# Experts in pairs: two sorted groups of 64 tokens as fp32 products in the two halves of TensorE's output rows

## The chip, the core and the metric

The kernel runs on one core of a Trainium2 chip. The metric is the time on the device in microseconds (us), median of several executions.

## What is computed

Two transformer layers and a third block over 512 tokens of width 1024, all in float32. Only the mixture of experts of the last block matters here. Each token goes to 2 of 32 experts, so there are 1024 pairs of token and expert. An expert is a SwiGLU layer with 256 hidden columns:

```python
expert_id = g_sel[:, None] * EXPERTS_PER_GROUP + top_i        # 2 of 32 for each token
hid = silu(h @ w_gate[e]) * (h @ w_up[e])                      # (tokens, 1024) x (1024, 256), twice
y   = sum over the token's two experts of weight * (hid @ w_down[e])
```

With the inputs that the kernel gets, the reference sends between 5 and 67 pairs to an expert. Two experts get more than 64 (numbers 17 and 19, with 65 and 67), none gets more than 128.

A second, small part of the change is in the retention layer: there each head's output is centred (its mean over 128 columns is taken off) before it is normalised.

## The kernel before

The kernel is one hand-scheduled program: each engine has its own list of instructions and semaphores join them. TensorE's products are mostly split: an fp32 matrix is divided into a high part, rounded to the fp32r type, and a low remainder, and `three` (L585 to L587) issues three fp32r products for one product. ScalarE makes the high parts, VectorE subtracts to get the low ones.

The mixture of experts works on tokens sorted by expert. A routing stage ranks the pairs, and products with a selection matrix gather the 1024 sorted places into `xs` (L1242, L1257; copied out by ScalarE, L1896). Then 39 blocks of `SLOTS` = 128 places follow: 32 blocks, one for each expert, and `XOVER` = 7 more for experts with over 128 pairs, whose number is read from a table when the kernel runs. A block takes its window of 128 places out of `xs` at an address read from `window_at`, which an over block and the places behind an expert's last pair share with others: results of places that are not the block's are not stored.

One block `it` is, by engine:

- SP queue (L530 to L558): three panels of weights of 1 MB each, two for gate and up (`moe_raw`) and one for down (`moe_down`). The panels sit in 2 x 2 and 3 buffers, and a load waits until TensorE is done with the buffer (`up_done`, `down_done`).
- ScalarE (L1858 to L1919): high parts of the two up panels and of half the down panel (`high_up`, `high_down`), the window's high part (`high_window`), silu, the copy of the transposed hidden values, the copy of the result to `y_out`.
- VectorE (L2729 to L2751, loop from L2844): the low parts, and silu(gate) x up into `xhid` (L2852).
- TensorE (L1263 to L1314): `up(it)`: 8 x 3 split products, with the 128 tokens stationary and 512 columns of weights streaming; `down_moe(it - 1)`: two plain fp32 products (L1294) for half of the 256 hidden rows and 2 x 3 split ones for the other half; `turn_hid(it)`: two transposes. Block 0 takes its window from `xw0_hi` and `xw0_lo`, which is places 0 to 127 and needs no table.
- GpSimd (L2996 to L3000): an indirect DMA stores the 128 rows of a block to their sorted places in `expert_out` in HBM; rows that are not the block's are given an address past the end and dropped.

Behind the blocks GpSimd fetches each token's two results (`back`), and a last gated layer follows (panels `A_PG`), beginning on TensorE with the products of `w_ple` (L1322).

In the retention layer, a head's output goes to `ry` (L2548), `mean_r` (L1111 to L1113) makes its mean with a product by ones, and `centred` (L2550 to L2556) subtracts it.

## Time and profile before

| | |
|---|---|
| median of 3 runs | 2317.38 us (2317.13 to 2322.71) |
| profiled execution, its own time | 2318.59 us |
| its span in the trace | 2316.8 us |
| TensorE busy | 2270.3 us, 98% |
| VectorE, ScalarE, GpSimd busy | 1549.1, 1066.8, 185.8 us |
| moved by DMA | 308.86 MB, mean 133 GB/s |

The span is the time between the first and the last instruction of the core; the execution's own time is 1.8 us longer. A matmul's record in the trace covers its way through the array too, so that records overlap: what one costs in a row of them is the distance between their starts. An fp32 product has two records, each with its own load of the stationary operand (PEld rows). "Idle before" is time in which the engine did nothing, with what ended it.

### The profile page before, as it was taken

The numbers are of one execution on the slowest core, as the hardware profiler recorded it, in microseconds if no ns is written. First come the engines' busy times: TensorE is split into PE (matmuls) and PEld (weight loads), VectorE is DVE, ScalarE is ACT, GpSimd is POOL, SyncE is SP. The second block draws the span as 40 slices with busy tenths as digits, with TensorE's granted clock in tenths as the row PEclk, the third lists the DMA queues.
The fourth block names the chain that finished last, engine by engine and source line by source line (L and its number), as shares of the span: only waits on it lengthen the run. The fifth ranks groups of instructions, "written<-read, shape, count | busy, mean of one in ns | idle before, by whom it ended". The sixth has DMA issues, their size and how long they took to land. (4 is left out here: it accounts for less than half of the span.)

```text
span 2316.8 us, 28797 instructions
## 1 busy us (share of the span) xinstructions
PE 2270.3 (98%) x10880; PEld 1848.0 (80%) x10880; DVE 1549.1 (67%) x1948; ACT 1066.8 (46%) x1351; POOL 185.8 (8%) x158
## 2 busy tenths in 40 slices
PE   8999999999999999999999999999999999999998
PEld 6787888888779779998788888777788877777766
DVE  6776855555687676664655555777654678888868
ACT  5556522222334345653422222645422368888863
POOL 1334200000100000000000000200000101110120
PEclk9999999999999999999999999999999999999999
DMA  4322222222133531003322322111221349999961
GB/s 184 109 88 77 109 100 95 95 108 82 68 127 123 172 108 35 29 28 112 119 106 84 109 87 94 55 73 55 104 87 64 140 163 371 372 371 375 365 235 55
DMA packets 56662, 308.86 MB, mean 133 GB/s; under 512 B 10204, under 2 KB 10588, under 8 KB 26608
## 3 DMA queue, kind: packets, MB, share of 16 engines
q1 hardware_dynamic: 44336, 280.51, 32.3%
q0 software_dynamic: 10976, 24.22, 3.3%
q10 hardware_dynamic: 1248, 2.75, 0.3%
q8 instruction: 66, 1.08, 0.2%
q14 instruction: 36, 0.29, 0.0%
HBM read 294.64 MB, written 29.00 MB: 140 GB/s over the span
## 5 line engine op out<-in xcount | busy, mean ns | idle before, releaser
L585 PE MATMUL psum<-hn_hi,a_hi 128*128 128x512 f32 (+1 forms) x1592 | 625.8, 393 | 9.1 <-DVE a_lo L1963 3.2
L587 PE MATMUL psum<-hn_hi,a_lo 128*128 128x512 f32 (+1 forms) x1592 | 618.5, 388 | 0.0
L586 PE MATMUL psum<-hn_lo,a_hi 128*128 128x512 f32 (+1 forms) x1592 | 618.0, 388 | 0.0
L585 PEld LDWEIGHTS psum<-hn_hi,a_hi 128*128 128x128 f32 (+1 forms) x1592 | 296.9, 187 | 78.3 <-issue 7.1
L586 PEld LDWEIGHTS psum<-hn_lo,a_hi 128*128 128x128 f32 (+1 forms) x1592 | 297.1, 187 | 64.8 <-issue 2.4
L587 PEld LDWEIGHTS psum<-hn_hi,a_lo 128*128 128x128 f32 (+1 forms) x1592 | 296.9, 187 | 64.0
L1963 DVE TENSOR_TENSOR a_lo<-a_raw,a_hi 128x2048 fp32r<-128x2048 f32 (+1 forms) x110 | 249.9, 2271 | 77.6 <-ACT a_hi L1371 77.1
L1371 ACT ACTIVATE a_hi<-a_raw 128x2048 fp32r<-128x2048 f32 (+1 forms) x110 | 205.9, 1874 | 66.9 <-PE psum L587 56.6
L2732 DVE TENSOR_TENSOR moe_lo<-moe_raw,moe_hi 128x2048 fp32r<-128x2048 f32 x78 | 178.3, 2287 | 2.9 <-ACT moe_hi L1863 2.5
L2047 DVE TENSOR_TENSOR h<-h,psum 128x512 f32<-128x512 f32 x176 | 119.4, 687 | 78.4 <-PE psum L587 78.4
L1533 ACT ACTIVATE sg<-sg 128x512 f32<-128x512 f32 x44 | 27.8, 632 | 286.3 <-DVE sg L2200 286.3
L1863 ACT ACTIVATE moe_hi<-moe_raw 128x2048 fp32r<-128x2048 f32 x78 | 149.0, 1912 | 1.1 <-PE psum L587 0.7
L585 PE MATMUL psum<-hid_hi,b_hi 128*128 128x512 f32 x352 | 137.3, 390 | 2.2 <-DVE h L2047 2.1
L587 PE MATMUL psum<-hid_hi,b_lo 128*128 128x512 f32 x352 | 137.0, 389 | 0.0
L586 PE MATMUL psum<-hid_lo,b_hi 128*128 128x512 f32 x352 | 137.0, 389 | 0.0
L585 PE MATMUL psum<-moe_hi,xw_hi 128*128 128x512 f32 x312 | 125.2, 401 | 2.2 <-DVE moe_lo L2732 2.2
L587 PE MATMUL psum<-moe_hi,xw_lo 128*128 128x512 f32 x312 | 121.6, 390 | 0.0
L586 PE MATMUL psum<-moe_lo,xw_hi 128*128 128x512 f32 x312 | 121.5, 390 | 0.0
L1535 ACT ACTIVATE hid_hi<-hid 128x512 fp32r<-128x512 f32 x44 | 27.8, 632 | 177.5 <-DVE hid L2205 177.5
L2205 DVE TENSOR_TENSOR hid<-sg,psum 128x512 f32<-128x512 f32 x44 | 30.3, 688 | 113.8 <-PE psum L587 113.7
L2926 POOL TENSOR_TENSOR sq<-sq 128x512 f32<-128x512 f32 x6 | 9.0, 1503 | 1132.6 <-ACT sq L1384 1132.6
L1378 ACT ACTIVATE b_hi<-b_raw 128x1024 fp32r<-128x1024 f32 x64 | 66.9, 1050 | 60.6 <-PE psum L587 58.4
(506 smaller groups left out, 3986.5 us busy)
## 6 DMA issues: line engine op xcount, KB each, us to landing
a_raw<-w_a SPq DMA_DIRECT2D x116, 1024.0 KB, 5.1
moe_raw<-w_m SPq DMA_DIRECT2D x78, 1024.0 KB, 7.7
moe_down<-w_m SPq DMA_DIRECT2D x39, 1024.0 KB, 7.9
b_raw<-w_b SPq DMA_DIRECT2D x64, 512.0 KB, 3.3
q_scratch<-qb POOLq DMA_DIRECT2D x8, 768.0 KB, 4.8
qs<-q_scratch POOLq DMA_DIRECT2D x16, 384.0 KB, 3.6
out_t<-h SPq DMA_DIRECT2D x7, 256.0 KB, 2.0
h<-x_t ACTq DMA_DIRECT2D x3, 512.0 KB, 8.8
```

The source lines that it names most:

```text
L585: pe.matmul(out, w_hi, x_hi, start=first, stop=False)
L586: pe.matmul(out, w_hi, x_lo, start=False, stop=False)
L587: return pe.matmul(out, w_lo, x_hi, start=False, stop=last)
L1371: act.activation(a_hi[s % 2][:, 0:w], a_raw[s % 2][:, 0:w], ACT.Copy).then_inc(a_rounded, 1)
L1378: act.activation(b_hi[s % 2][:, :], b_raw[s % 2][:, :], ACT.Copy).then_inc(b_rounded, 1)
L1533: act.activation(sg[:, f, :], sg[:, f, :], ACT.Silu).then_inc(gate_done, 1)
L1535: act.activation(hid_hi[:, f, :], hid[:, f, :], ACT.Copy).then_inc(hid_rounded, 1)
L1863: act.activation(moe_hi[c][:, :], moe_raw[v][c][:, :], ACT.Copy).then_inc(moe_rounded, 1)
L1963: V.tensor_tensor(a_lo[s % 2][:, 0:w], a_raw[s % 2][:, 0:w], a_hi[s % 2][:, 0:w], ALU.subtract) \
L2047: V.tensor_tensor(h[:, m, :], h[:, m, :], bank[4 + m % 4][:, :], ALU.add).then_inc(y_free, 1)
L2205: V.tensor_tensor(hid[:, f, :], sg[:, f, :], ps[1][:, :], ALU.mult).then_inc(tile_free, 2)
L2732: V.tensor_tensor(moe_lo[v][c][:, :], moe_raw[v][c][:, :], moe_hi[c][:, :], ALU.subtract) \
```

## The change

Two experts are worked on at the same time, expert n and expert n + 16, with 64 places each. The 64 places of the first are the lower half of the stationary operand and of the output rows, those of the second the upper half. All their products are plain fp32: nothing is split, and the window is one tile `xw`. A step `s` is such a pair: 16 "main" steps for the 32 experts and 8 "over" steps for up to 16 further blocks of experts with more than 64 pairs, in the order main, over, main, eight times. All 24 steps are always worked through.

The panels of the main steps, 96 of them, pass through a ring of 8 buffers, loaded by SP in the order of their use. The panels of the over steps have two buffers for each half and are fetched by GpSimd with an indirect DMA, whose row numbers `over_row` come from a table; where there is no over block, 127 of the 128 rows get a number past the end and are not fetched. ScalarE copies the window of the first half (`window_a`), VectorE that of the second (`window_b`). Stores are one for each step.

In the retention layer the mean is taken off the values `rv` instead (`values_centred`: a reduction over each token's columns and a subtraction), and `mean_r`, `centred` and the tile `ry` go; the output is copied straight to `ryc`.

The core of the diff. Of lines removed only those of the constants and of `mean_r` are shown; the others are in the functions printed above.

```diff
-XBLOCKS = EXPERTS + (2 * S - EXPERTS) // SLOTS
-XOVER = XBLOCKS - EXPERTS
+SLOTS = 64
+XHALF = EXPERTS // 2
+XOVER = 16
+XCOLS = XHALF + XOVER // 2
+XBLOCKS = 2 * XCOLS
 PAIRS = 2 * S
...
+NSTEP = len(STEPS)
+PANELS = 8
+def _panel_order():
+    up_at, down_at, order = {}, {}, []
+    for s in range(NSTEP + 1):
+        if s < NSTEP and STEPS[s][0] == "main":
+            up_at[s] = len(order)
+            order += [(STEPS[s][1] + XHALF * half, c) for c in range(2) for half in range(2)]
+        if s and STEPS[s - 1][0] == "main":
+            down_at[s - 1] = len(order)
+            order += [(STEPS[s - 1][1] + XHALF * half, 2) for half in range(2)]
+    return up_at, down_at, order
+UP_AT, DOWN_AT, PANEL_ORDER = _panel_order()
+def column(s):
...
+        def half_of(half):
+            return slice(half * SLOTS, (half + 1) * SLOTS)
+        def after_up(s):
+            kind, n = STEPS[s]
+            return (main_used, UP_AT[s] + 4) if kind == "main" else (over_used, 6 * n + 4)
+        def after_down(s):
+            kind, n = STEPS[s]
+            return (main_used, DOWN_AT[s] + 2) if kind == "main" else (over_used, 6 * n + 6)
         block = ctx.enter_context(nc.Block())
         ds = bass.ds
...
+                    sp.wait_ge(main_used, n - PANELS + 1)
...
-            def mean_r(i):
-                pe.wait_ge(r_y, i + 1)
-                pe.matmul(bank[2][:, :], ones, ry[:, :], start=True, stop=True).then_inc(r_mean, 1)
...
+            def weights(s, c):
+                kind, n = STEPS[s]
+                w = []
+                for half in range(2):
+                    if kind == "main":
+                        at = (UP_AT[s] + 2 * c if c < 2 else DOWN_AT[s]) + half
+                        i = at % PANELS
+                        pe.wait_ge(panel_loaded[i], 16 * (at // PANELS) + (32 if i < 4 else 16))
+                        w.append(panel[i])
+                    else:
+                        q = 3 * n + c
+                        pe.wait_ge(over_loaded[half][q % 2], 16 * (q // 2) + 16)
+                        w.append(over_panel[half][q % 2])
+                return w, main_used if kind == "main" else over_used
+            def up(s):
+                v = s % 2
+                pe.wait_ge(xwa_ready, s + 1)
+                pe.wait_ge(xwb_ready, s + 1)
+                if s >= 2:
+                    pe.wait_ge(xhid_done, s - 1)
                 for k in range(KT):
                     if k % 4 == 0:
+                        w, used = weights(s, k // 4)
+                    for half in range(2):
+                        rows = half_of(half)
+                        mm = pe.matmul(bank[v][rows, :], xw[:, v, k, rows],
+                                       w[half][:, k % 4 * 2 * EFF:(k % 4 + 1) * 2 * EFF], start=k == 0, stop=k == KT - 1)
+                        if k % 4 == 3:
+                            mm.then_inc(used, 1)
+            def turn_hid(s):
+                v = s % 2
+                pe.wait_ge(xhid_done, s + 1)
+                if s >= 2:
+                    pe.wait_ge(xturn_done, s - 1)
                 for f in range(2):
+                    mm = pe.transpose(bank[2 + v][:, f * P:(f + 1) * P], xhid[:, v, f * P:(f + 1) * P], ident)
                 mm.then_inc(xturn_mm, 1)
+            def down_moe(s):
+                v = s % 2
+                pe.wait_ge(xturn_done, s + 1)
+                if s >= 2:
+                    pe.wait_ge(y_copied, s - 1)
+                w, used = weights(s, 2)
                 for hb in range(2):
+                    for f in range(2):
+                        for half in range(2):
+                            rows = half_of(half)
+                            mm = pe.matmul(bank[4 + 2 * v + hb][rows, :],
+                                           xturn[:, v, f * P + half * SLOTS:f * P + (half + 1) * SLOTS],
+                                           w[half][:, f * D + hb * 512:f * D + (hb + 1) * 512],
+                                           start=f == 0, stop=f == 1)
+                            if hb == 1 and f == 1:
+                                mm.then_inc(used, 1)
+            pe.wait_ge(xs_copied, 2 * KT)
             up(0)
             up(1)
             turn_hid(0)
             down_moe(0)
             turn_hid(1)
+            for s in range(2, NSTEP):
+                up(s)
+                down_moe(s - 1)
+                turn_hid(s)
+            down_moe(NSTEP - 1)
...
+            def window_a(s):
+                if s >= 2:
+                    act.wait_ge(*after_up(s - 2))
+                c = column(s)
...
+            def values_centred(i):
+                V.wait_ge(v_turned, 2 + i)
+                x = bank[0][:, :].rearrange("p (t c) -> p t c", t=NT)
+                step(V.tensor_reduce(rm[:, :], x, AX_X, ALU.add))
+                V.scalar_tensor_tensor(rv[:, :].rearrange("p (t c) -> p t c", t=NT),
+                                       rm[:, :].rearrange("p (t o) -> p t o", o=1).to_broadcast([P, NT, P]), -1.0 / P, x,
+                                       ALU.mult, ALU.add).then_inc(tile_free, 1)
...
+            def window_b(s):
+                if s >= 2:
+                    V.wait_ge(*after_up(s - 2))
+                c = XCOLS + column(s)
...
+            step(V.scalar_tensor_tensor(over_at[:, 0, :], xov[:, 0, :], 3.0 * P,
+                                        cnc("row", 1).to_broadcast([P, XOVER]), ALU.mult, ALU.add))
+            step(V.tensor_scalar(over_at[:, 1, :], xov[:, 2, :], -1.0, 1.0, ALU.mult, ALU.add))
+            step(V.scalar_tensor_tensor(over_at[:, 0, :], over_at[:, 1, :], cnc("skip", 1), over_at[:, 0, :],
+                                        ALU.mult, ALU.add))
+            for c in range(2):
+                step(V.tensor_scalar(over_row[:, c, :], over_at[:, 0, :], float(c * P), None, ALU.add))
...
+            V.wait_ge(xs_copied, 2 * KT)
+            window_b(0)
...
             sums(T_MOE)
+            def load_over(q):
+                o, c = q // 3, q % 3
+                if q >= 2:
+                    pool.wait_ge(over_used, 2 * q - 2)
+                for half in range(2):
+                    j = half * (XOVER // 2) + o
+                    pool.indirect_dma_start(
+                        over_panel[half][q % 2][:, :], None, w_m.rearrange("a p n -> (a p) n"),
+                        bass.IndirectOffsetOnAxis(ap=over_row[:, c, j:j + 1], axis=0),
+                        bounds_check=3 * EXPERTS * P - 1, oob_is_err=False).then_inc(over_loaded[half][q % 2], 16)
+            def store_y(s):
+                c = column(s)
+                pool.wait_ge(y_copied, s + 1)
+                pool.indirect_dma_start(
+                    y_dram[:, :], bass.IndirectOffsetOnAxis(ap=y_row[:, c:c + 1], axis=0), y_out[:, s % 2, :], None,
+                    bounds_check=PAIRS + XBLOCKS - 1, oob_is_err=False).then_inc(y_stored[s % 2], 16)
...
+            for s in range(NSTEP):
+                kind, o = STEPS[s]
+                if kind == "over":
+                    load_over(3 * o + 2)
+                    if o + 1 < XOVER // 2:
+                        load_over(3 * o + 3)
+                    store_y(s - 1)
+                    if o + 1 < XOVER // 2:
+                        load_over(3 * o + 4)
+                    store_y(s)
+                    store_y(s + 1)
+            pool.wait_ge(xwa_ready, NSTEP)
+            pool.wait_ge(xwb_ready, NSTEP)
...
```

## Rows read from the trace of the kernel before

**Rows 1.** The page, busy time of each engine over the whole span.
```profile
PE 2270.3 (98%) x10880; PEld 1848.0 (80%) x10880; DVE 1549.1 (67%) x1948; ACT 1066.8 (46%) x1351; POOL 185.8 (8%) x158
```

**Rows 2.** The windows: busy us (x count) per engine, clock, DMA share, GB/s.
```profile
1840.00:1850.00 10.00, 10.00 (x57) 9.09 (x56) 8.86 (x35) 4.02 (x5) 0.00 (x0) 0.83 1.01 426
...
2000.00:2050.00 50.00, 50.00 (x209) 37.78 (x208) 43.55 (x42) 41.13 (x41) 5.77 (x6) 1.00 0.97 366
2150.00:2200.00 50.00, 50.00 (x210) 37.80 (x209) 44.06 (x42) 40.98 (x41) 5.76 (x6) 1.00 0.97 365
```

**Rows 3.** Groups by line, 1884.4 to 2235.1 us: xcount | busy, mean ns | idle before.
```profile
L2732 DVE TENSOR_TENSOR moe_lo<-moe_raw,moe_hi 128x2048 fp32r<-128x2048 f32 x76 | 173.8, 2287 | 2.9 <-ACT moe_hi L1863 2.5
...
L1294 PE MATMUL psum<-moe_down,xturn 128*128 128x512 f32 x156 | 73.4, 593 | 1.6 <-ACT xturn L1875 1.6
...
L2998 POOL DMA_INDIRECT expert_out<-y_out,y_row x38 | 38.9, 1023 | 306.4 <-ACT y_out L1888 298.2 <-issue 8.2
...
L1912 ACT ACTIVATE xsg<-psum 128x256 f32<-128x256 f32 x39 | 14.9, 383 | 27.9 <-PE psum L587 27.8
```

**Rows 4.** The timeline of TensorE, one block: start us, us, engine, line, operands.
```profile
2001.44 0.48 PE L585 MATMUL psum<-moe_hi,xw_hi 128*128 128x512 f32 x1
2001.76 0.39 PE L586 MATMUL psum<-moe_lo,xw_hi 128*128 128x512 f32 x1
...
2006.77 0.39 PE L587 MATMUL psum<-moe_hi,xw_lo 128*128 128x512 f32 x1
2007.00 1.88 PE L1294 MATMUL psum<-moe_down,xturn 128*128 128x512 f32 x4
...
2009.87 0.39 PE L587 MATMUL psum<-moe_down_hi,xturn_lo 128*128 128x512 f32 x1
2010.10 0.38 PE L1284 MATMUL psum<-cn,xhid 128*128 128x128 f32 x2
2010.24 0.48 PE L585 MATMUL psum<-moe_hi,xw_hi 128*128 128x512 f32 x1
```

**Rows 5.** The waits of the SP queue, 1900 to 2200 us: us, times, longest.
```profile
SPq L537 <- PE psum L587: 164.6, 67, 4.9
SPq L545 <- PE psum L587: 94.2, 34, 3.9
```

**Rows 6.** DMA issues, 1900 to 2200 us: KB each, median us to landing.
```profile
moe_raw<-w_m SPq DMA_DIRECT2D x67, 1024.0 KB, 7.8
```

**Rows 7.** The timeline of TensorE around a product with 64-column stationaries.
```profile
1521.80 0.39 PE L587 MATMUL psum<-hn_hi,a_lo 128*128 128x512 f32 x1
1522.12 1.74 PE L1086 MATMUL psum<-wpt,sv 128*64 128x128 f32 x14
```

**Rows 8.** The timeline where the expert stage begins.
```profile
1884.41 0.39 PE L585 MATMUL psum<-moe_hi,xw_hi 128*128 128x512 f32 x1
...
1884.61 0.60 ACT L1896 ACTIVATE xs<-psum 128x512 f32<-128x512 f32 x1 [1.22 <-PE psum L1257]
...
1886.13 1.06 ACT L1870 ACTIVATE xw_hi<-xs 128x1024 fp32r x1 [0.93 <-ACT xs L1896]
...
1891.81 0.47 PE L585 MATMUL psum<-moe_hi,xw_hi 128*128 128x512 f32 x1 [1.80 <-DVE moe_lo L2732]
...
1892.12 0.40 PE L586 MATMUL psum<-moe_lo,xw_hi 128*128 128x512 f32 x1
```

**Rows 9.** The timeline of TensorE where the expert stage ends.
```profile
2231.39 1.98 PE L1294 MATMUL psum<-moe_down,xturn 128*128 128x512 f32 x4 [1.17 <-ACT xturn L1875]
...
2235.14 1.45 PE L1322 MATMUL psum<-ptr,w_ple 128*128 128x512 f32 x3
```

**Rows 10.** The timeline of the retention stage, one head.
```profile
1541.29 0.68 DVE L2628 COPY rv<-psum 128x512 f32<-128x512 f32 x1
...
1558.36 1.02 PE L1113 MATMUL psum<-ry,cn 128*128 128x512 f32 x2
...
1559.31 1.74 PE L1086 MATMUL psum<-wpt,sv 128*64 128x128 f32 x14
```

More of the change, by code:

```diff
@@ L46 @@
 NO_ROW = 8192
+NO_WEIGHT = 16384
+STEPS = [(kind, n) for o in range(XOVER // 2) for kind, n in (("main", 2 * o), ("over", o), ("main", 2 * o + 1))]
+NSTEP = len(STEPS)
[13 more added lines that the diff above has]
+    kind, n = STEPS[s]
+    return n if kind == "main" else XHALF + n
 WA, WB = 2048, 1024
@@ L97 @@
           ("cmp_mask", NT * NCMP), ("prio_g", NT * EGROUPS), ("prio_e", NT * EPG),
-          ("upto", P), ("iota", S), ("step", XOVER), ("past", XOVER),
-          ("lane", 1), ("spare", XBLOCKS)]
+          ("upto", P), ("iota", S), ("past", XOVER),
+          ("lane", 1), ("row", 1), ("skip", 1), ("spare", XBLOCKS)]
 def _columns(parts):
@@ L196, in build @@
         with ExitStack() as st:
-            moe_raw = [[sb(f"moe_raw{c}{v}", [P, WA], F32, st) for c in range(2)] for v in (1, 0)][::-1]
-            moe_hi = [sb(f"moe_hi{c}", [P, WA], F32R, st) for c in range(2)]
-            moe_down = [sb(f"moe_down{v}", [P, WA], F32, st) for v in range(3)]
-        with ExitStack() as st:
-            moe_lo = [[sb(f"moe_lo{c}{v}", [P, WA], F32R, st) for c in range(2)] for v in (1, 0)][::-1]
-            sb("over_moe_hi", [P, 2, WA], F32, st)
-            moe_down_lo = [sb(f"moe_down_lo{v}", [P, 2, D], F32R, st) for v in range(3)]
+            panel = [sb(f"panel{i}", [P, WA], F32, st) for i in range(PANELS)]
+            over_11 = sb("over_panel11", [P, WA], F32, st)
         with ExitStack() as st:
@@ L1156, in _ @@
                     out_r(i - 1)
-                if k % 4 == 1 and 0 < i <= RET_H:
-                    mean_r(i - 1)
                 if k % 4 == 2 and 0 < i <= RET_H:
@@ L1283, in turn_hid @@
+            def turn_hid(s):
[3 more added lines that the diff above has]
+                    pe.wait_ge(xturn_done, s - 1)
                 for f in range(2):
-                    mm = pe.transpose(bank[2 + v][:, f * SLOTS:(f + 1) * SLOTS], xhid[:, v, f * P:(f + 1) * P], ident)
+                    mm = pe.transpose(bank[2 + v][:, f * P:(f + 1) * P], xhid[:, v, f * P:(f + 1) * P], ident)
                 mm.then_inc(xturn_mm, 1)
-            def down_moe(it):
-                v = it % 2
-                pe.wait_ge(xturn_done, it + 1)
-                pe.wait_ge(down_loaded[it % 3], 16 * (it // 3) + 16)
-                if it >= 2:
-                    pe.wait_ge(y_copied, it - 1)
-                for hb in range(2):
-                    pe.matmul(bank[4 + 2 * v + hb][:, :], xturn[:, v, 0:SLOTS],
-                              moe_down[it % 3][:, hb * 512:(hb + 1) * 512], start=True, stop=False)
-                pe.wait_ge(moe_split, down_split(it))
-                for hb in range(2):
-                    c = slice(hb * 512, (hb + 1) * 512)
-                    mm = three(bank[4 + 2 * v + hb][:, :], xturn_hi[:, v, :], xturn_lo[:, v, :],
-                               moe_down_hi[:, c], moe_down_lo[it % 3][:, 1, c], False, True)
-                mm.then_inc(down_done, 1)
@@ L1309, in _ @@
             turn_hid(1)
-            for it in range(2, XBLOCKS):
-                up(it)
-                down_moe(it - 1)
-                turn_hid(it)
-            down_moe(XBLOCKS - 1)
+            for s in range(2, NSTEP):
[3 more added lines that the diff above has]
+            down_moe(NSTEP - 1)
             pe.wait_ge(table_loaded, 96)
@@ L1888, in copy_y, with copy_turned @@
+            def copy_turned(s):
+                v = s % 2
+                act.wait_ge(xturn_mm, s + 1)
+                act.activation(xturn[:, v, :], bank[2 + v][:, 0:EFF], ACT.Copy).then_inc(xturn_done, 1)
+            def copy_y(s):
+                v = s % 2
+                act.wait_ge(*after_down(s))
+                if s >= 2:
+                    act.wait_ge(y_stored[v], 16 * (s // 2))
                 act.activation(y_out[:, v, :].rearrange("p (b c) -> p b c", b=2), psum[:, 4 + 2 * v:6 + 2 * v, :],
@@ L2804, in _ @@
             step(V.tensor_scalar(over, count, SLOTS + 0.5, None, ALU.is_ge))
-            for n in (2, 3):
+            for n in range(2, S // SLOTS):
                 step(V.scalar_tensor_tensor(over, count, n * SLOTS + 0.5, over, ALU.is_ge, ALU.add))
@@ L3167, in _constants @@
     put("iota", np.tile(np.arange(S), (P, 1)))
-    put("step", np.tile(np.arange(XOVER), (P, 1)))
     put("past", np.tile(SLOTS * (1 + np.arange(XOVER)), (P, 1)))
-    put("lane", r[:, None])
+    put("lane", r[:, None] % SLOTS)
+    put("row", r[:, None])
+    put("skip", np.where(r[:, None] == 0, 0, NO_WEIGHT))
     put("spare", np.where(r[:, None] == 0, PAIRS + np.arange(XBLOCKS)[None, :], NO_ROW))
```

259 lines of the change are left out of this document (77 added, 182 removed).

## The prediction

> **What bounds the kernel now.** I read the page first: TensorE is busy 98% of the span [rows 1], so a change counts by what it does to TensorE's queue. The table of windows places the expert stage: 1884.4 us (first product of block 0) to 2235.1 us (the row behind the last one) [rows 8, 9], 350.7 us for 39 blocks of 128 places. In it TensorE is at 50.00 of 50 us at full clock (2.4 GHz), VectorE at about 44, and the DMA engines at a share of 0.97 with 365 to 366 GB/s [rows 2]: two resources near their end, so I had to see which sets the pace. The timeline shows block after block without a hole: up products from 2001.44 to 2007.00, the two fp32 down products and six split ones to 2010.10, the transposes to 2010.24, where the next block starts [rows 4]. That is 8.80 us a block, and in the waits TensorE hardly waits for anything, while the SP queue stands 164.6 and 94.2 us waiting for TensorE to free panels [rows 5]. TensorE sets the pace; the DMAs follow, landing 7.8 us after issue [rows 6].
>
> Prices on TensorE, from the same rows. Record durations overlap, so I go by starts. A split (fp32r) product of 512 columns follows the last by 0.23 us. An fp32 product is two records, each 0.43 us behind the last (four records in 1.88 us, the last 0.59 long) [rows 4, 3]: 0.86 us. So three split products cost 0.69 us, one fp32 product 0.86.
>
> **The change, part by part.**
> Up: a step now has two halves of 64 places, 8 x 2 fp32 products of 512 columns. Down: 2 x 2 x 2 of them. 24 fp32 products are 12 pairs, the two of a pair in different column halves of the array. Everything hangs on the price of a pair: 0.86 us if the halves run beside each other, 1.72 if they queue. No row of before shows two such halves side by side. What rows do show: an fp32 record takes 0.43 us for 512 values, an fp32r record reads the same bytes in 0.23 [rows 4], so the read path has room for two fp32 streams; and 64-column stationaries in a column half already run in the kernel (14 records in 1.74 us, 0.113 apart [rows 7]), though never alternating. Against it: the loads. Today each load hides behind the running product; with alternating halves, the load of the next half can sit behind a product that waits. An exposed 128-column load costs 0.08 us (1891.81 to 1892.12 is 0.31 instead of 0.23) [rows 8]. A pair has two changes of half, so it costs 0.86 to 1.02. I take 0.94, since a 64-column load should expose about half of 0.08.
>
> Above 0.86 the Trainium skill bears on this. "TensorEngine Tiling" (Key Properties) says that different tiles can execute their loads and matmuls in parallel; no row here shows that. "TensorE: Matmul & The Clock Gate" (Part 3) gives three column tiles as 2.38 times faster, 79% of ideal; as an estimate that makes a pair 1.09 us and the sum about 2291 us, the third rival's time.
>
> Transposes stay (0.14 us plus 0.09 for the longer gap behind them [rows 4]); a change between whole-array and half-array products showed 0.32 us where 0.23 is usual [rows 7], so twice 0.09. Together 0.42. Step: 12 x 0.94 + 0.42 = 11.70 us; 24 steps (16 main, 8 over, the empty ones too) 280.8 us.
>
> Removed on VectorE and ScalarE: all splitting of weights (2.29 us per panel on VectorE [rows 3]); two window copies of half the size stay. Neither engine bounds the stage, so this buys nothing by itself. The chain silu (0.38 us [rows 3]), product, transpose, copy still fits beside the down products of the step before.
>
> Start: block 0 used to start straight behind the gathering product, from xw0. Now step 0 waits for the last xs copy (ends 1885.21) and a window copy. The old one started at 1886.13 and took 1.06 us for twice the size [rows 8]: about 0.6 now, so step 0 starts near 1886.9, 2.5 us later (0 to 3). In exchange the hole of 1.80 us in block 1 [rows 8] goes; it is within the 350.7. End: the wait for xturn before the last down product (1.17 us [rows 9]) stays, with some 0.2 of load: 1.4. So the stage ends at 1886.9 + 280.8 + 1.4 = 2169.1 instead of 2235.1: 66 us less.
>
> Weights: 96 ring panels instead of 117. Eight load early, as the nine did. A panel is 1.049 MB: 2.46 us at the 426 GB/s of the first burst, 2.87 us at the 366 GB/s of the steady stage [rows 2]. Two experts exceed 64 places, so only two of the 16 over places are real: six panels, two of them loaded before step 0; the other 42 indirect loads fetch one row each. 88 + 4 panels at 2.87 us are 264 us from the first freed pair (1886.9 + 3.8 = 1890.7), so the last lands at 2155, and its down product ends 3.8 us later: 2159, ten before TensorE. Within a cycle of three steps (35.1 us) the ring asks for 12 panels, 34.4 us of stream; the ring holds four pairs, and going through a cycle's order of use by hand, a freed pair of slots is needed again after 14 us or more, where landing takes 7.8 [rows 6]. It fits, closely. What is late next, were TensorE faster, is the stream: at 0.86 us a pair the cycle is 32.2 us and the DMAs bind unless they go at the burst's rate.
> "DMA: Bandwidth & Descriptors" of the Trainium skill (Specifications) puts HBM at about 358 GB/s per core; as an estimate that makes a panel 2.93 us and the stream's end 2165, still ahead of TensorE. The 426 GB/s row disagrees with that limit.
>
> GpSimd: 48 indirect weight loads and 24 stores at 1.02 us [rows 3], 73 us spread over 281. A store waits behind load_over, which waits for over_used; those waits end when the over step's own products do, before the y they delay is ready. For an over place, the down panel is asked for half-way through up and needed one step later: some 13 us against 7.8. Nothing. The added small VectorE operations before step 0 lie beside the gathering products: nothing, at worst 2 us.
>
> Retention: four fp32 mean products go (0.95 us from the start of one to the next row [rows 10]); VectorE exchanges a copy of rv (0.68 us [rows 10]) for a reduction and a subtraction, and loses one pass later. The later release of the bank could give some back: 0 to 3.8 us gained, I take 3.4, since TensorE is the bound there too.
>
> **Sum.** The profiled execution took 2318.59 us; 2318.6 - 66.0 - 3.4 = 2249.2. It lies 1.2 above the median of the runs (2317.4), so 2248 us. With pairs at 0.86 the step is 10.74, the stage ends at 2146.1: 2225. With pairs at 1.02 it is 12.66, ends at 2192.1: 2271.
>
> **Rivals.**
> B, the halves don't run beside each other: a pair costs 1.72, a step 12 x 1.72 + 0.42 = 21.06, the stage 505, ending at 2393.7: 158.6 - 3.4 slower, 2473 us, though the DMAs idle. For it: no row shows two halves at once, and TensorE's records here always stream one behind the other. Against: the read path has the room. It decides above 1.20 us a pair (14.4 + 0.42 = 14.8 a step, 356 us): there the gain is gone.
> C, half overlap: every load waits, so a record costs 0.43 + 0.113 [rows 7] and a pair twice that, 1.09: step 13.5, stage end 2212, 2291 us. Against it: in the trace products of one row group follow 0.23 apart although a load of 188 ns lies between them [rows 4], so loads do hide today. "TensorE: Matmul & The Clock Gate" (Part 3) says that loads overlap products only when the row group differs, which would mean this rival; by that rule the trace disagrees for whole-array products, and halves are open.
> D, the stream becomes the bound: the ring drains in two main steps in a row, and the stream idles when it is full. If it idles 5 us in each of the eight cycles, a cycle is 39.5 us, the stage 316: 2283 us. For it: the share of 0.97 today [rows 2]. Against: the burst's 426 GB/s.
>
> **How the numbers follow.** Forecast 0.66, B 0.18, C 0.10, D 0.06. The likeliest case's own range is 2225 to 2271. The range takes in C and D with their spread and leaves out B: 2220 to 2330. Within 0.3% (7 us, about what a measurement here can tell from nothing) only a mixture lands: 0.02. Faster is the forecast, D and C less that sliver, 0.80; slower is B, 0.18.
>
> **What would show it.** Right: starts of the new up products 0.43 to 0.5 us apart per two records, 16 products in about 7.5 us; TensorE's rows without long waits; SP still waiting for TensorE; steps of 11.7 us. Records 0.43 apart each, a step of 21 us: B. Each load ended before its product starts, pairs of 1.09: C. TensorE waiting for DMA panel at the second main step of a cycle: D. A hole of more than 3 us before step 0, or a y_out that waits for its store, would be costs that I put at nothing.

## The result, and the profile after

The changed kernel takes 2258.88 us (median of 4 runs, 2255.83 to 2263.06), the kernel before beside it on the same chip 2320.05 us (4 runs): a ratio of 0.974, 95% interval 0.972 to 0.975, 61 us less. The forecast was 2248 us. The profiled execution took 2255.83 us, its span is 2254.0 us.

The page of the changed kernel: the busy line that answers to [rows 1], the throughput of the 40 slices (the five from 412 to 240 GB/s are most of the expert stage), and the costliest group of the expert stage.

```profile
PE 2199.1 (98%) x10668; PEld 1678.9 (74%) x10668; DVE 1275.3 (57%) x1733; ACT 841.8 (37%) x1174; POOL 219.5 (10%) x191
...
GB/s 189 90 97 94 112 75 112 84 106 90 93 70 141 145 159 51 35 29 49 152 79 112 84 106 89 93 57 57 57 112 84 66 144 198 412 408 393 388 240 57
...
L1297 PE MATMUL psum<-panel,xw 128*64 128x512 f32 x512 | 115.2, 603 | 2.4 <-ACT xw L1887 2.4
```

VectorE loses 274 us and ScalarE 225 us of work, and neither matters. What matters is TensorE's timeline. One step in the steady part, which answers to [rows 4] (start us, us, then the operands and the records in the group):

```profile
2008.88 7.09 PE L1297 MATMUL psum<-over_panel,xw 128*64 128x512 f32 x32
2015.80 3.60 PE L1321 MATMUL psum<-panel,xturn 128*64 128x512 f32 x16
2019.33 0.44 PE L1308 MATMUL psum<-cn,xhid 128*128 128x128 f32 x2
2019.70 0.65 PE L1297 MATMUL psum<-panel,xw 128*64 128x512 f32 x2
```

From 2008.88 to 2015.80 are 32 records, that is 16 fp32 products or eight pairs, in 6.92 us: 0.865 us a pair, which is what one whole-array fp32 product cost before. A record lasts 0.60 us ("603" in the group above) as it did for the whole array [rows 3], but on average one starts every 0.22 us instead of every 0.43 [rows 4]: the starts come in twos, 0.006 us apart, and the next two follow 0.43 us later (the second two of a group 0.48). The whole step is 2019.70 - 2008.88 = 10.82 us.

The stage begins at 1892.35 and ends at 2171.68. The rows of the timeline that are not like the one above, of 24 steps, with what ended the wait ahead of each in brackets:

```profile
1892.35 8.79 PE L1297 MATMUL psum<-panel,xw 128*64 128x512 f32 x32 [2.39 <-ACT xw L1887]
...
1908.84 3.65 PE L1321 MATMUL psum<-panel,xturn 128*64 128x512 f32 x16 [0.47 <-ACT xturn L1892]
...
1927.03 5.39 PE L1321 MATMUL psum<-over_panel,xturn 128*64 128x512 f32 x16 [7.15 <-DMA over_panel<-w_m,over_row]
...
1961.65 3.65 PE L1321 MATMUL psum<-over_panel,xturn 128*64 128x512 f32 x16 [0.20 <-DMA over_panel<-w_m,over_row]
...
2039.73 5.35 PE L1321 MATMUL psum<-panel,xturn 128*64 128x512 f32 x16 [2.01 <-DMA panel<-w_m]
...
2107.23 3.65 PE L1321 MATMUL psum<-panel,xturn 128*64 128x512 f32 x16 [0.66 <-DMA panel<-w_m]
...
2141.38 3.65 PE L1321 MATMUL psum<-panel,xturn 128*64 128x512 f32 x16 [1.47 <-DMA panel<-w_m]
...
2168.10 3.65 PE L1321 MATMUL psum<-panel,xturn 128*64 128x512 f32 x16 [1.06 <-ACT xturn L1892]
2171.68 14.00 PE L1346 MATMUL psum<-ptr,w_ple 128*128 128x512 f32 x32
```

24 steps of 10.82 us are 259.7 us; the stage takes 279.3. The 19.6 us between them are, by these rows: 7.7 us for over panels, 4.9 us for ring panels, 1.9 us for xturn at the two ends, and 5.2 us in three groups that last 1.7 to 1.8 us longer than their like (8.79 instead of 7.09, 5.39 and 5.35 instead of 3.60). The windows of two of those three show why. Columns as in [rows 2]; the clock is the last but two:

```profile
1927.00:1931.00 4.00, 3.97 (x12) 1.38 (x14) 0.00 (x0) 0.00 (x0) 0.00 (x0) 0.55 1.02 424
2000.00:2020.00 20.00, 20.00 (x94) 6.57 (x92) 1.70 (x4) 3.86 (x7) 6.94 (x7) 1.00 1.02 413
2040.00:2044.00 4.00, 4.00 (x12) 1.28 (x10) 0.00 (x0) 0.00 (x0) 0.00 (x0) 0.60 1.03 413
```

Behind a hole of 7.15 and one of 2.01 us TensorE's granted clock is mostly at its lower level (1.2 GHz) for some microseconds, and at full level where it never stopped. So a wait for a panel can cost itself and 1.8 us more; behind the waits of 0.66 and 1.47 us the products run at their usual pace.

The longest wait comes from GpSimd. Its timeline at the start of the stage:

```profile
1895.47 0.99 POOL L2993 DMA_INDIRECT over_panel<-w_m,over_row  x1 [0.30 <-issue]
1896.46 0.78 POOL L3009 DMA_DIRECT2D ptr<-p_t  x1
1897.22 0.76 POOL L3010 DMA_DIRECT2D w_ple<-w_p  x1
1897.94 0.57 POOL L3011 DMA_DIRECT2D expert_out<-h  x1
1914.18 1.04 POOL L2993 DMA_INDIRECT over_panel<-w_m,over_row  x1 [15.68 <-DMA expert_out<-h]
```

The down panel of over place 0 could have been asked for at 1897. But the program has GpSimd wait first until the tables and the rows that fill expert_out's spare places have landed, 15.68 us with DMA engines that are full of panels, and the down panel, asked for from 1914.18, is what TensorE waits 7.15 us for.

Outside the stage the kernel is the same but for the retention part, and yet the last gathering product ends its queue 5.4 us later than before (1889.57 against 1884.18), although the retention part should have brought it forward. Windows of stretches in which the two programs are the same, first of the kernel before:

```profile
200.00:600.00 400.00, 396.93 (x1746) 327.17 (x1745) 238.03 (x270) 126.98 (x138) 21.18 (x15) 1.00 0.26 96
...
1150.00:1450.00 300.00, 300.00 (x1325) 248.51 (x1324) 160.59 (x183) 76.08 (x75) 0.00 (x0) 1.00 0.26 94
```

and of the changed kernel:

```profile
200.00:600.00 400.00, 397.45 (x1731) 324.99 (x1731) 236.36 (x268) 127.20 (x139) 21.33 (x15) 1.00 0.25 94
...
1150.00:1450.00 300.00, 300.00 (x1312) 246.49 (x1311) 160.49 (x183) 74.01 (x73) 0.00 (x0) 1.00 0.27 98
```

TensorE is busy for all of the 300 us in both, at full clock, and gets 1312 instead of 1325 products done: each follows the last 1% later. One thing that the change touches there is the layout: the tile of constants grows from 1460 to 1473 words per partition, with its filler from 5888 to 5952 bytes, and everything laid out behind it moves by 64 bytes. Among it are hn_hi and hn_lo, the streaming operands of these products; their stationary operands (a_hi, a_lo) lie ahead of the constants and stay.

### The profile page after: what moved, and what is told of

The parts are those of the page before. It is cut to its first block, busy times and chain, and to the rows that moved or that the text cites. A ratio compares the mean times of both kernels' runs of the same rounds, so it can differ in the third digit from the quotient of the medians.

```text
span 2254.0 us, 27637 instructions
## 1 busy us (share of the span) xinstructions
PE 2199.1 (98%) x10668; PEld 1678.9 (74%) x10668; DVE 1275.3 (57%) x1733; ACT 841.8 (37%) x1174; POOL 219.5 (10%) x191
## 4 chain that ended last, share of the span: by engine, by line
PE 78%; DVE 9%; DMA 5%; ACT 4%; issue 3%; POOL 1%; ACTq 0%; SPq 0%; POOLq 0%; DVEq 0%
PE psum L598 20%; PE psum L600 20%; PE psum L599 20%; PE psum L1297 5%; PE psum L997 3%; PE psum L1321 3%; DMA panel<-w_m 2%; PE psum L961 2%; DVE xc L2096 1%; ACT a_hi L1395 1%; DMA over_panel<-w_m,over_row 1%; PE psum L1264 1%; DVE a_lo L1967 1%; DMA expert_out<-h 1%; PE psum L923 1%
## 5 line engine op out<-in xcount | busy, mean ns | idle before, releaser
L2850 DVE TENSOR_TENSOR xhid<-xsg,psum 128x256 f32<-128x256 f32 x24 | 10.1, 422 | 240.4 <-ACT xsg L1917 240.4
L1297 PE MATMUL psum<-panel,xw 128*64 128x512 f32 x512 | 115.2, 603 | 2.4 <-ACT xw L1887 2.4
L1297 PEld LDWEIGHTS psum<-panel,xw 128*64 128x64 f32 x512 | 36.5, 138 | 69.9 <-issue 69.9
L1973 DVE TENSOR_TENSOR b_lo<-b_raw,b_hi 128x1024 fp32r<-128x1024 f32 x64 | 80.1, 1258 | 7.1 <-ACT b_hi L1402 7.1
L997 PE MATMUL psum<-vn,pt 128*128 128x65 f32 x640 | 82.0, 275 | 0.0
```

The lines of the kernel that those rows point to most:

```text
L997: mm = pe.matmul(o(1 + b), pt[:, v, c, at + k * P:at + (k + 1) * P], vn[:, b, k, g, :], start=k == 0, stop=k == t)
L1297: mm = pe.matmul(bank[v][rows, :], xw[:, v, k, rows], w[half][:, k % 4 * 2 * EFF:(k % 4 + 1) * 2 * EFF], start=k == 0, stop=k == KT - 1)
L1973: V.tensor_tensor(b_lo[s % 2][:, :], b_raw[s % 2][:, :], b_hi[s % 2][:, :], ALU.subtract) \
```

## The experiments

**The layout, undone in the changed kernel.** The constant "skip" is dropped and computed by one instruction from "row"; the tile's size in memory, and so every address behind it, is again that of before.

```diff
-          ("lane", 1), ("row", 1), ("skip", 1), ("spare", XBLOCKS)]
+          ("lane", 1), ("row", 1), ("spare", XBLOCKS)]
...
-                step(V.scalar_tensor_tensor(over_at[:, 0, :], over_at[:, 1, :], cnc("skip", 1), over_at[:, 0, :],
+                step(V.tensor_scalar(skip[:, :], cnc("row", 1), 0.5, float(NO_WEIGHT), ALU.is_ge, ALU.mult))
+                step(V.scalar_tensor_tensor(over_at[:, 0, :], over_at[:, 1, :], skip[:, :], over_at[:, 0, :],
```

> The changed kernel with one constant column less, so that every tile allocated behind the constants (hn_hi, hn_lo, hid_hi and the rest) lies at the same byte address as in the kernel before, 64 bytes lower than in the changed one; one small VectorE operation makes the column's values instead. Theory (address): in the changed kernel the unchanged split products ran 0.4% slower (111 instead of 112 in 25 us), because of that shift; with the addresses back, the product of 1500 us where nothing was changed comes 7.5 us earlier and the whole is about 2249 to 2251 us. Rival (chip or run): the slower products belong to the execution, not to the addresses; the time stays at 2256 to 2259 us.

Measured: 2247.49 us (2246.61 to 2247.62), ratio to the kernel before 0.969 (0.967 to 0.971); 11.4 us less than the changed kernel (8.4 between the two profiled executions), and a little below what was expected. The first window holds as many products as before:

```profile
200.00:600.00 400.00, 396.95 (x1745) 327.02 (x1745) 237.74 (x270) 127.15 (x139) 21.18 (x15) 1.00 0.26 96
```

The stage starts at 1883.22. Undoing a shift of 64 bytes gives back all of the 1%.

**The layout, moved in the kernel before.** The other way round, with nothing of the change:

```diff
         cn = sb("cn", [P, N_CONST])
+        sb("shift", [P, 16], fill=False)
```

> The kernel before with an unused tile of 64 bytes behind the constants, so that all later tiles lie 64 bytes higher, as in the changed kernel. Theory (address): 6 to 9 us slower than before, 2324 to 2328 us. Rival (chip or run): no change, 2317 to 2320 us.

Measured: 2334.91 us, ratio 1.007 (1.005 to 1.009); 15.6 us more. 1732 and 1313 products in the two windows, those of the changed kernel within one. So the shift alone does it; its size was expected at half of this. The last gathering product comes 8.3 us later (1892.43), as expected; the expert stage of the kernel before, whose split products I had left out, ends 13.2 us later (2248.37), so 5 us arise in it. The trace shows where: there the split products follow each other every 233.2 ns instead of 227.6, and 39 blocks of 24 such products at 5.6 ns more are 5.2 us.

**Other distances.** A shift of 128 bytes would have been the next to try; it doesn't fit into the memory, which has room for 96. Two runs with `[P, 8]` and `[P, 24]` in place of `[P, 16]`, 32 and 96 bytes:

> The kernel before with an unused tile of 32 bytes per partition behind the constants. The constants take 5856 bytes, so the tiles behind them, which are nearly all multiples of 128 bytes, begin 96 bytes into a stretch of 128; in the 64-byte shift they began 32 bytes into one. With 32 bytes they begin on a multiple of 128. If the cost of 64 bytes is one of the place within a stretch of 128 bytes, this run tells a third point of it: 2319 or less if a start on the multiple is no worse, 2335 if only the 96 is good. If both 96 and 32 are bad against 0, it is faster than the kernel before.

> As the last, with 96 bytes: the tiles begin 64 bytes into a stretch of 128. If any shift costs, whatever its size, 2335 as with 64 bytes. If the starts at 0 and 64 behave alike (a matter of 64 bytes), this run equals the last one. If the cost is one of distance, it lies above 2335.

Measured: 2359.03 us with 32 bytes, ratio 1.017 (1.015 to 1.018), and 2359.88 us with 96, ratio 1.017 (1.015 to 1.019). The window of 200 to 600 us, of the run with 32 bytes

```profile
200.00:600.00 400.00, 398.54 (x1703) 318.71 (x1702) 232.25 (x264) 127.15 (x139) 21.90 (x16) 1.00 0.26 95
```

and of the run with 96:

```profile
200.00:600.00 400.00, 398.53 (x1704) 319.16 (x1703) 231.28 (x263) 127.27 (x138) 21.52 (x15) 1.00 0.25 94
```

So it isn't the distance (96 bytes cost what 32 do, 64 cost less than half), and not any shift alike. The run with 32 bytes came out as none of the three cases expected of it; the one with 96 equals it, the second of its own. The recorded text on 32 bytes also counts the start of the tiles wrongly: the helper `sb` of the kernel fills each tile up to a multiple of 64 bytes, so that the constants take 5888 bytes and not 5856. Counted through the program's tiles, the operands behind the constants (hn, hid, sel, nat and the xw of before) begin on a multiple of 128 bytes in the kernel before, 64 past one in the changed kernel and in the first shift, and 32 and 96 past one in these two runs. The best place is the multiple of 128, 64 past it is a middling one, 32 and 96 are bad.

Which operand it is, the traces tell in part. The mean distance between the starts of neighbouring split products (ns, without gaps over 290), where "moved" says which operand lies behind the constants:

| products | moved | before | changed kernel | 64 bytes | 32 bytes | 96 bytes |
|---|---|---|---|---|---|---|
| a (stationary), hn (streaming) | streaming | 227.1 | 229.0 | 229.1 | 233.3 | 233.3 |
| xw (stationary), moe (streaming) | stationary | 227.6 | none | 233.2 | 233.1 | 234.1 |
| nat (stationary), sel (streaming) | both | 227.3 | 226.8 | 227.1 | 227.5 | 227.5 |

Either operand can do it, and where both moved by the same bytes the pace stayed. That fits a cost of two operands that begin at different places within 128 bytes; no run moved one tile alone, so this is read from the traces and not shown. The plain fp32 products of the changed kernel's stage show nothing of it (10.82 us a step in either layout). Whether the pattern repeats after 128 bytes was not tried.

**GpSimd's waits moved behind the over loads.**

```diff
-            pool.wait_ge(table_loaded, 96)
-            pool.wait_ge(tables_ready, 4)
             for s in range(NSTEP):
                 kind, o = STEPS[s]
                 if kind == "over":
                     load_over(3 * o + 2)
                     if o + 1 < XOVER // 2:
                         load_over(3 * o + 3)
+                    if o == 0:
+                        pool.wait_ge(table_loaded, 96)
+                        pool.wait_ge(tables_ready, 4)
```

> The changed kernel, with GpSimd issuing the third and fourth load of the over panels before it waits for the tables and for the filling of the store's spare rows. Theory (order on GpSimd): TensorE's longest wait in the expert stage, 7.15 us for the first over down panel, came from that order, and the cold clock behind it cost 1.8 us more; both go, and the kernel is 8 to 9 us faster, about 2247 to 2250 us. Rival (bandwidth): the indirect load is slow because the ring and the tables fill the DMA engines; the wait shrinks by less than half and the time stays above 2253 us.

Measured: 2255.61 us (2254.32 to 2256.29), ratio 0.973 (0.971 to 0.974), 3.3 us less than the changed kernel, which is not clear of the spread of the runs (the two intervals overlap), and the stage only 1.0 us shorter (278.3). TensorE's waits in the stage, first of the changed kernel (us in total, times, longest):

```profile
PE psum L1321 <- DMA over_panel<-w_m,over_row: 7.3, 2, 7.2
PE psum L1321 <- DMA panel<-w_m: 4.1, 3, 2.0
PE psum L1297 <- ACT xw L1887: 2.4, 1, 2.4
PE psum L1321 <- ACT xturn L1892: 1.5, 2, 1.1
```

and of this run:

```profile
PE psum L1321 <- DMA panel<-w_m: 8.6, 6, 2.0
PE psum L1321 <- DMA over_panel<-w_m,over_row: 2.7, 1, 2.7
PE psum L1297 <- ACT xw L1887: 2.4, 1, 2.4
PE psum L1297 <- DMA panel<-w_m: 2.0, 2, 1.7
...
PE psum L1297 <- DMA over_panel<-w_m,over_row: 1.2, 1, 1.2
```

11.4 us of waiting for panels in five places before, 14.5 in ten places now. The low clock is gone as well, which the window of the stage shows (the changed kernel's has a clock of 0.97, below):

```profile
1890.00:2120.00 230.00, 213.38 (x978) 71.84 (x978) 21.30 (x55) 47.08 (x81) 63.46 (x64) 1.00 0.99 398
```

So the time is the rival's, but not for the rival's reason: the wait for the first over down panel did shrink by more than half (7.15 to 2.69 us), and 5.2 us of low clock went too. 1.0 us of that is left in the stage. A wait that is removed and comes back as others of the same kind points to the stream of weights, not to the order on GpSimd.

**A quarter of each panel.** The changed kernel with both edits above, and with only the first quarter of every ring panel loaded, but for the first eight; the remaining columns keep what the ring held. The experts' products therefore use wrong weights; their number, sizes and order are the same.

```diff
-                sp.dma_start(panel[n % PANELS][:, :], w_m[3 * e + c]).then_inc(panel_loaded[n % PANELS], 16)
+                cols = slice(0, WA if n < PANELS else WA // 4)
+                sp.dma_start(panel[n % PANELS][:, cols], w_m[3 * e + c][:, cols]).then_inc(panel_loaded[n % PANELS], 16)
```

> The changed kernel with one constant column less and the over loads first; besides, of every panel behind the first eight only a quarter of the columns is loaded (the products run on what lies in the rest, so the experts' results are left wrong). TensorE's work is the same, the weight stream is cut to about a third. Theory (the stream now binds): with the stream out of the way no wait for a panel is left, the stage takes 24 x 10.82 = 260 us and 3 to 5 us of filling and end, and the kernel about 2229 to 2233 us. Rival (TensorE and its own cold clock bind): the stage stays at 270 us or more, the kernel above 2238 us.

Measured, in a single execution: 2228.66 us, just below the range of the theory. The stage takes 261.5 us (1883.60 to 2145.14), and all of TensorE's waits in it are these:

```profile
PE psum L1299 <- ACT xw L1889: 2.4, 1, 2.4
PE psum L1323 <- ACT xturn L1894: 1.5, 2, 1.1
```

With both edits and the whole panels (next), the same stage takes 279.5 us. The stream costs 18 us, of which some 3 are the low clock behind a wait of 3.11 us for an over panel (16 down records in 6.60 us instead of 3.65).

**Both edits together, and with TensorE kept busy before step 0.** The second run adds five small products ahead of the wait for xs (`keep(7, 5)` before `pe.wait_ge(xs_copied, 2 * KT)`).

> The changed kernel with one constant column less and the over loads first. By the two runs before, the first is worth 11 us; the second removes a wait of 9 us but the stream gives most of it back. Theory (stream binds): 2244 to 2246 us, 1 to 4 less than with one column less alone. Rival (the waits add up): 2238 us.

> The same with five small products on an unused bank ahead of step 0, which keep TensorE busy while it waits for the windows. Theory (cold clock): the 3.4 us at 1.2 GHz behind the 2.4 us hole go, step 0's up takes 7.1 us instead of up to 8.8, and the kernel gains up to 1.7 us where the stream lets it. Rival (stream binds): the time of the run beside it, within 1 us.

Measured: 2246.91 us (2243.55 to 2252.55), ratio 0.969 (0.967 to 0.971), and 2246.37 us (2245.68 to 2248.31), ratio 0.969 (0.967 to 0.970). Neither differs from the layout alone (2247.49), so the second edit is worth nothing here; the waits didn't add up to the rival's 2238. The filling products turned the hole of 2.4 us into one of 0.23, and the wait for an over panel in the next step grew from 1.6 to 2.0 us. But step 0's up took 7.09 us in both runs: without the filling products the clock behind the hole was at its full level already, so there was nothing to win, and the run doesn't test its theory.

**A ring of six.** `PANELS = 6`, with an unused tile in the place of the two panels, so that nothing else moves.

> The changed kernel with six panels in its ring instead of eight (the two panels' room is kept by an unused tile, so addresses stay). If the stream binds the stage because it stands still whenever the ring is full and TensorE then outruns it, a smaller ring stands still longer: more and longer waits of TensorE for DMA panel than the changed kernel's, the stage 5 to 25 us longer, 2264 to 2284 us, with fewer GB/s than the 396 of the changed kernel. If the DMA engines' rate alone bound it, without the ring, the ring's size would change only the two panels less loaded ahead: 2 x 2.6 us, 2264 at most. If the stream doesn't bind, 2259 as before.

Measured: 2266.37 us (2259.87 to 2274.25), ratio 0.978 (0.975 to 0.981), 7.5 us more than the changed kernel; the stage takes 284.5 us (1891.86 to 2176.34), 5.2 more. The windows from 1890 to 2120 us of the changed kernel

```profile
1890.00:2120.00 230.00, 217.16 (x976) 72.53 (x978) 21.32 (x55) 47.08 (x81) 63.40 (x64) 0.97 0.99 396
```

and of this one:

```profile
1890.00:2120.00 230.00, 212.12 (x952) 70.42 (x954) 20.47 (x53) 45.57 (x79) 60.47 (x61) 0.97 0.97 388
```

The 5.2 us in the stage are what the two panels less that lie ready when it starts would cost (2 x 2.6 us at 400 GB/s). The signs of a ring that stands still are there, but small: 388 instead of 396 GB/s, and nine waits for panels instead of five. This trace is of the fastest of four executions that lie over 14 us apart (2259.87 to 2274.25), and the slower ones have none. In the traced execution a ring that stands still was at most a minor cost; for the others it stays open.

**The halves in turn instead of alternating.** Per pair of panels, four products of the lower half and then four of the upper; number and operands are the same.

```diff
-                for k in range(KT):
-                    if k % 4 == 0:
-                        w, used = weights(s, k // 4)
+                for c in range(2):
+                    w, used = weights(s, c)
                     for half in range(2):
                         rows = half_of(half)
-                        mm = pe.matmul(...)
-                        if k % 4 == 3:
-                            mm.then_inc(used, 1)
+                        for k in range(4 * c, 4 * c + 4):
+                            mm = pe.matmul(...)
+                        mm.then_inc(used, 1)
```

> The changed kernel with the up products in another order: for each pair of panels first the four products of the lower half, then the four of the upper half, instead of by turns. Same products, same result. Theory (alternation): two halves run beside each other only where a product of one follows a product of the other; then of 16 products only the ones at a change of half overlap, an up takes 12 to 14 us instead of 6.9, and the kernel about 2400 us (24 x 5 to 7 us more). Rival (queueing by bank or by half doesn't matter): the up stays near 6.9 us and the time near 2256.

Measured, in a single execution: 2291.75 us, 33 us more than the changed kernel, which is neither of the two times expected. A step, from TensorE's timeline:

```profile
2000.19 7.68 PE L1297 MATMUL psum<-panel,xw 128*64 128x512 f32 x29
2007.29 0.64 PE L1321 MATMUL psum<-over_panel,xturn 128*64 128x512 f32 x1
2007.71 0.59 PE L1297 MATMUL psum<-panel,xw 128*64 128x512 f32 x1
2007.77 0.59 PE L1321 MATMUL psum<-over_panel,xturn 128*64 128x512 f32 x1
...
2008.63 3.97 PE L1321 MATMUL psum<-over_panel,xturn 128*64 128x512 f32 x13
2012.53 0.44 PE L1308 MATMUL psum<-cn,xhid 128*128 128x128 f32 x2
2012.89 1.50 PE L1297 MATMUL psum<-panel,xw 128*64 128x512 f32 x3
```

12.70 us a step instead of 10.82. The down products of the lower half start 0.06 us beside up products of the upper one: a half that has nothing to do takes work that stands further on, here even of the next loop. How far, the starts at the head of the step tell: the lower half's first four records stand alone (at 0.00, 0.48, 0.91 and 1.34 us), and with its fifth, at 1.77, the upper half's first starts, 0.006 us later. That one is the ninth in the queue, so a half reached four records (two products) ahead and no further. So the halves need not alternate product by product, but it costs 1.88 us a step if they don't. 24 steps make 45 us; the stage takes 311.2 us, 31.9 more, since what lies between the steps shrinks from 19.6 to 6.4 us. Waits for ring panels are gone: at 12.70 us a step TensorE sets the pace, not the stream.

**The retention part alone,** in the kernel before: the four mean products go, and rv is centred as it is copied.

```diff
-                        V.wait_ge(v_turned, 2 + i)
-                        V.tensor_copy(rv[:, :], bank[0][:, :]).then_inc(tile_free, 1)
+                        values_centred(i)
...
-                if k % 4 == 1 and 0 < i <= RET_H:
-                    mean_r(i - 1)
```

> The kernel before with the retention part of the change alone (the mean taken off rv, no product by ones). Forecast of the prediction: 3.4 us faster, about 2314 to 2316 us. Rival (bank released later): nothing or slower, 2317 to 2320 us.

Measured: 2315.78 us, ratio 0.9987 (0.9978 to 0.9997), 3.6 us less than the kernel before beside it (by the interval 0.7 to 5.1).

## Why the prediction came out as it did

The forecast's mechanism held, and its time was 11 us too low (2248 against 2258.9). That is a small sum of large errors in both directions, so that it came so near is luck. On the stage's end the forecast said 2169.1 - 3.4 = 2165.7; the trace says 2171.7. By terms:

- **The pair of fp32 products, 0.94 us: too dear.** It is 0.865 us, the lower end of the bounds; the load of the next half hides entirely. The step of 11.70 us is 10.82, and 24 of them take 21.1 us less. I had added half of an exposed load, and took its size from a load behind a hole [rows 8], where nothing was running that could hide it; in a row of products loads are hidden [rows 4], and so they are here. "TensorEngine Tiling" (Key Properties) of the Trainium skill says that different tiles run their loads and products in parallel; this trace agrees, with 0.865 us for two instead of 1.72. The loss that the prediction worked out from the three column tiles of "TensorE: Matmul & The Clock Gate" (Part 3) of the Trainium skill (2.38 of 3, or 79%) isn't seen here: 1.72 / 0.865 is 1.99 of 2. Nor does that section's rule that a load overlaps a product only when the row group differs hold for two column halves, which use all rows: each pair would then have cost the 1.09 us of rival C.
- **Rival B** is out by the same number. The run with the halves in turn shows that the order counts, and how much.
- **The start, 1886.9 less 3.4 = 1883.5 us: right, but for the layout.** Step 0 starts 1.76 us after the last xs copy ends (1890.59 to 1892.35), where I had 1.7. In the run with the old layout it starts at 1883.22. What moved it to 1892.35 is the 64 bytes. No step of the prediction dealt with the products before the stage: that a column of constants could change the rate of over 6,000 unchanged products wasn't among the terms, and none of the rivals had it. It costs 11.4 us here by the medians (8.4 between the profiled executions); the other errors nearly cancel.
- **GpSimd, "Nothing": wrong.** I priced the queue behind load_over and behind the stores, but not the wait for table_loaded and tables_ready that stands ahead of the first down panel's load, and I took 7.8 us for a landing in a queue where that transfer took 15.5 us. It shows as 7.15 us of TensorE's waiting and 1.8 more at the lower clock. Yet taking both away returns 1.0 us of the stage, and 0.2 in the old layout (279.8 to 279.5): it was a real wait, and hardly a real cost.
- **The stream, "ten us before TensorE": wrong, and the reason the last point costs nothing.** The step says that at 0.86 us a pair "the DMAs bind unless they go at the burst's rate"; that is what happened. The DMAs go at 396 GB/s, near the burst. But I gave all of that rate to the ring: the queue that carries over panels, tables and stores takes 12 of the 91 MB in this stretch, and the ring gets 343 GB/s, 3.06 us a panel instead of 2.87. The queues of the changed kernel from 1890 to 2120 us (packets, MB, share of the 16 engines' time):

```profile
q1 hardware_dynamic: 10835, 78.96, 83.5%
q0 software_dynamic: 8832, 12.02, 14.9%
```

  96 panels less the eight loaded early, at 3.06 us from 1896.2 (the first freed pair), are 2165.5, and 3.8 us for the last one's products make 2169: within 3 us of the end that was measured. Rival D named what happened, the stream as the bound, and its sign is in the trace: the three waits for ring panels all stand ahead of the down products of the second main step of a cycle. It cost not 5 us per cycle but 18 us in all, by the run with a quarter of each panel. The way that D gave for it did not: the DMA engines hardly idle (share 0.99), and it is their rate, shared with the other queue, against a cheaper pair. The 358 GB/s of "DMA: Bandwidth & Descriptors" (Specifications) of the Trainium skill did not bound this kernel: the trace shows 396 over 230 us and up to 424 in a window. The prediction called that a disagreement, but the same page (Measured, under Bandwidth) gives 425 for a core whose neighbour is idle and 358 as the share when both stream; this kernel runs on one core, and the trace agrees with that.
- **Retention, 3.4 us less: right,** 3.6 measured.
- **What wasn't priced: the clock.** Three stretches at the lower level cost 5.2 us in the changed kernel. Two of them follow waits for panels. The run with GpSimd's waits moved has none of the three and a stage only 1.0 us shorter, so the stream takes most of them back.

The terms put together: +8.9 for the start, -21.1 for the steps, +18.2 for what lies between them (19.6 instead of 1.4) are the 6.0 us by which the stage's end was missed. The stretch behind it takes 0.6 us more than before (82.3 against 81.7), and the median lies 3.1 us above the profiled execution where I had it 1.2 below: together the 11 us.

Three kernels beat the changed one by over 11 us with the layout of before: 2247.5 us with one constant less, 2246.9 with both edits and 2246.4 with the filling products too, all 0.969 of the kernel before. What is left to gain in the stage is the stream's 18 us. The two changes of order that were tried gave nothing of it; fewer bytes did, though no run tried that with the right weights.

## What to carry to other kernels

Two half-width fp32 products in the two column halves cost what one does, loads and all, if they stand side by side in the queue; with groups of few rows this was worth more here than splitting the weights to save passes (two experts in 10.82 us instead of 17.6). When a change makes the busiest engine cheaper, add up the next resource with everything that shares it, not only with the transfer in question: here 24 steps are 260 us on TensorE and the 88 panels 269 us in the stream, and removing single waits then moves next to nothing. And compare the rate of unchanged stretches first: a tile that grows by some bytes moves all that is laid out behind it, and here that cost as much as a planned improvement brings.

## What the runs showed of the hardware that was not expected

- Where the tiles behind the constants begin sets the pace of the split products that use them with an operand that stayed: with the same program 1746, 1732, 1703 and 1704 products in the same 400 us for shifts of 0, 64, 32 and 96 bytes, and 2319, 2335, 2359 and 2360 us for the kernel. Products whose two operands moved alike kept their 227 ns.
- Two records in different column halves run fully beside each other, 0.6 us each and 0.22 us apart on average (32 in 6.92 us), and a half takes work that stands up to four records (two products) ahead of what the other is at.
- The hole ahead of a stretch didn't alone decide the clock behind it: after 2.39 us the first up group took 8.79 us in the changed kernel (8.62 in the ring of six, after 2.40), and 7.09 us after the same 2.39 or 2.40 in the three runs with the old layout, but also in the one with GpSimd's waits moved, which has the new layout. So it isn't the layout; why the clock fell in some and not in others stays open.
